# An RWKV-7 core in four steps: key products moved inside each level, level 0 of the inverse taken as a masked copy of L

## The reference, cut to what matters

```
def step(state, inp):                       # wkv7_scan, inside lax.scan
    r_t, w_t, k_t, v_t, a_t, b_t = inp
    sa = jnp.einsum('bhvk,bhk->bhv', state, a_t)
    state = state * w_t[:, :, None, :] + sa[..., None] * b_t[:, :, None, :] + v_t[..., None] * k_t[:, :, None, :]
    y = jnp.einsum('bhvk,bhk->bhv', state, r_t)
    return state, y
y_f, bonus_f = direction(0); y_b, bonus_b = direction(1)
y = y_f + y_b
```

## Time and profile before

| what | value |
|---|---|
| median of three executions | 1351.7 us |
| the profiled execution, its own time | 1352.12 us |
| its span in the profile | 1350.0 us |
| PE busy | 1307.8 us, 97% |
| PEld busy | 999.6 us, 74% |
| DVE busy | 883.9 us, 65% |
| ACT busy | 351.5 us, 26% |
| POOL busy | 120.7 us, 9% |
| granted clock of TensorE, mean | 0.995 |

### The profile page before, as it was taken

The page is one execution under the profiler, slowest core; times in us unless marked ns, Lnnn a source line. Parts: engine busy times, 40 slices in busy tenths (PEclk is TensorE's granted clock), DMA queues, the critical chain, the costliest instruction groups (busy, mean ns, idle before and its releaser), DMA issues.

```text
span 1350.0 us, 25515 instructions
## 1 busy us (share of the span) xinstructions
PE 1307.8 (97%) x11020; PEld 999.6 (74%) x11020; DVE 883.9 (65%) x1486; ACT 351.5 (26%) x756; POOL 120.7 (9%) x184
## 2 busy tenths in 40 slices
PE   7999999999999998999999999998989999999999
PEld 6868649599995444579997467846777765999943
DVE  4577762567878347558898577558444464798973
ACT  2311211212221024413332013703432341233300
POOL 5755000000000001010000000031000000000000
PEclk9989999999999999999999999999999999999999
DMA  8433252334544624044544533400011043354452
GB/s 328 157 133 133 109 187 99 130 126 169 187 162 158 251 84 156 0 179 165 188 165 155 214 153 125 187 1 3 4 35 34 21 170 125 126 188 175 146 184 88
DMA packets 16736, 182.34 MB, mean 135 GB/s; under 512 B 1648, under 2 KB 3952, under 8 KB 6000
## 3 DMA queue, kind: packets, MB, share of 16 engines
q1 hardware_dynamic: 14320, 175.12, 34.9%
q10 hardware_dynamic: 2304, 5.59, 1.1%
HBM read 179.65 MB, written 1.05 MB: 134 GB/s over the span
## 4 chain that ended last, share of the span: by engine, by line
PE 93%; DVE 4%; issue 1%; ACT 1%; DMA 0%; POOL 0%; DVEq 0%; POOLq 0%
PE banks L1722 28%; PE banks L1739 15%; PE banks L1432 11%; PE banks L1399 10%; PE banks L1409 4%; PE banks L2037 3%; PE banks L2026 2%; PE banks L1616 2%; PE banks L1687 2%; PE banks L1385 2%; DVE weight_ring L3140 1%; PE banks L2172 1%; PE banks L1881 1%; PE banks L2044 1%; DVE arena L3140 1%
## 5 line engine op out<-in xcount | busy, mean ns | idle before, releaser
L1722 PE MATMUL banks<-xn,arena 128*128 128x128 f32 x1440 | 165.7, 275 | 0.0
L1722 PEld LDWEIGHTS banks<-xn,arena 128*128 128x128 f32 x1440 | 163.2, 192 | 0.0
L1739 PE MATMUL banks<-arena 128*128 128x512 f32 x264 | 122.0, 592 | 0.0
L1722 PE MATMUL banks<-hT,weight_ring 128*128 128x128 f32 x960 | 116.5, 275 | 0.0
L1722 PEld LDWEIGHTS banks<-hT,weight_ring 128*128 128x128 f32 x960 | 111.8, 192 | 0.0
L1432 PE MATMUL banks<-weight_ring,arena 128*128 128x512 f32 x224 | 97.8, 593 | 0.8 <-ACT arena L1322 0.8
L1739 PEld LDWEIGHTS banks<-arena 128*128 128x128 f32 x264 | 49.8, 190 | 60.7 <-issue 60.7
L1739 PE MATMUL banks<-weight_ring,arena 128*128 128x512 f32 x198 | 93.3, 592 | 0.0
L2733 DVE SCALAR_TENSOR_TENSOR arena<-arena,prm 128x255 f32<-128x255 f32 x200 | 87.3, 479 | 5.4 <-ACT arena L1076 3.6
L1432 PEld LDWEIGHTS banks<-weight_ring,arena 128*128 128x128 f32 x224 | 42.2, 190 | 51.4 <-issue 49.7
L1076 ACT ACTIVATE arena<-arena,prm 128x256 f32<-128x256 f32 x100 | 54.6, 593 | 86.3 <-issue 44.2
(11 more groups left out here) (455 smaller groups left out, 2188.4 us busy)
## 6 DMA issues: line engine op xcount, KB each, us to landing
weight_ring<-in_wall SPq DMA_DIRECT2D x81, 2048.0 KB, 7.5
weight_ring<-in_wall SPq DMA_DIRECT2D x2, 1024.0 KB, 7.3
x<-in_x_tok ACTq DMA_DIRECT2D x2, 512.0 KB, 4.5
arena<-in_mem_tok SPq DMA_DIRECT2D x1, 1024.0 KB, 17.3
arena<-in_wall SPq DMA_DIRECT2D x1, 1024.0 KB, 5.1
arena<-in_wide SPq DMA_DIRECT2D x2, 512.0 KB, 5.1
out_y<-x ACTq DMA_DIRECT2D x4, 256.0 KB, 2.0
arena<-in_masks ACTq DMA_DIRECT2D x1, 896.0 KB, 9.6
```

Source lines behind the costliest of these rows:

```text
L1722: ins = mm(b_(n)[:, j * P:(j + 1) * P], lhsT=weights[:, kb, j * P:(j + 1) * P], rhs=features_[:, kb, :], start=opens and j == 0 and kb == ...
L1739: ins = mm(b_(n), lhsT=a, rhs=b, start=pair == 0, stop=pair == FB // 2 - 1)
```

## The change

In steps 1 to 3, level 0 is no longer computed by TensorE. VectorE writes the masked L directly into the turned T (`Tt`, set to the identity by GpSimd) with eight predicated copies of 64 x 256, TensorE turns it (`tw`) and ScalarE evicts the result into Tc. Level 1 then has no `tt`. The key products ab{j}1.. move from behind `tl` to between `yl` and `tl` of levels 1 to 3 (the fourth behind `tl` of level 4, in step 3 of level 3). VectorE copies `tl` of that level ahead of that product. `s_out` moves into level 4 between `yl` and `tl`; y_out(2,0) and gate(0) likewise in step 3. One product of the following step goes between `yl` and `tl` of level 5, in step 0 too, the other stays behind `tl`. The two `bk` pieces of a step go to levels 0 and 1 of the next one, gate(1) to level 0 of step 3. The core of the diff:

```
+def level_opens(j, lv):
+    return [(f"{x}{j}{lv}{h}", 1, "pair") for x in (("tt",) if lv > 1 else ()) + ("yl",) for h in HALVES]
+def level_closes(j, lv):
+    return [(f"tl{j}{lv}{h}", 1, "pair") for h in HALVES]
+def later_step(j, lv):
+    if lv == 0:
+        out = turned_keys(j - 1, 0) if j < 3 else [("gate1", 1, "pair")]
+        return out + tail_groups(j - 1, "xs") + [(f"tw{j}{h}", 1, "pair") for h in HALVES]
+    opens, closes, keys = level_opens(j, lv), level_closes(j, lv), key_products(j, 1, 0) + key_products(j, 1, 2)
+    if lv < 4:
+        out = opens + [keys[lv - 1]] + closes + [keys[3]] * (j == 3 and lv == 3) + tail_groups(j - 1, TAIL_AT[lv])
+        return out + (turned_keys(j - 1, 1) if lv == 1 and j < 3 else [])
+    if lv == 4:
+        y0, y1 = tail_groups(j - 1, "ys")
+        if j == 3:
+            return opens + [y0] + closes + [y1]
+        return opens + tail_groups(j - 1, "ss") + closes + [keys[3], y0] + key_products(j + 1, 0, 0) + [y1]
+    if j == 3:
+        return opens + [("gate0", 1, "pair")] + closes + [("ty1", 1, "pair")]
+    one, two = key_products(j + 1, 0, 2)
+    return opens + [one] + closes + [two]
...
+            def first_level(j, h):                                   # VectorE
+                d = STEPS[j][0]
+                dve.wait_ge(t_identity, 2 * j + h + 1)
+                for pp in range(2):
+                    dve.wait_ge(*when_read(G[f"ab{j}0{h}{pp}"]))
+                L = heads(LA[d][h])
+                m0 = MSK_DIR * (1 - d) + 512
+                for swap in (0, 1):
+                    for r in (0, 1):
+                        mask = masks[SIDE[r], m0:m0 + HD].unsqueeze(1).to_broadcast([HD, 4, HD])
+                        ins = V.copy_predicated(Tt[h][SIDE[r ^ swap], r], mask, L[SIDE[r], 4 * swap:4 * swap + 4, 0, SIDE[r ^ swap]])
+                ins.then_inc(first_level_made, 1)
...
+                    if j == 0 or lv:                                 # VectorE's list
+                        level(j, lv)
+                    if j and 0 < lv < 4:
+                        products(j, 1, (lv - 1) // 2, (lv - 1) % 2)
+                    if j < 3 and lv == 5:
+                        products(j + 1, 0, 1, 0)
...
+            def first_turn(j, h):                                    # TensorE
+                n = G[f"tw{j}{h}"]
+                free(n)
+                pe.wait_ge(first_level_made, 2 * (j - 1) + h + 1)
+                turn(n, Tt_rows[h])
...
+                    level_opens(j, lv)                               # TensorE's list
+                    if j and 0 < lv < 4:
+                        products(j, 1, (lv - 1) // 2, (lv - 1) % 2)
...
+                    if j < 3 and lv == 5:
+                        products(j + 1, 0, 1, 0)
...
+                    level_closes(j, lv)
...
-                    pool.wait_ge(psum_full, G[f"tf{j - 1}{h}"] + 1)
-                    g.tensor_copy(Tc[h], unit).then_inc(t_identity, 1)
+                    pool.wait_ge(psum_full, G[f"tl{j - 1}{LEVELS - 1}{h}"] + 1)
+                    g.tensor_copy(Tt[h], unit).then_inc(t_identity, 1)
```

More of the change, by code:

```diff
@@ L150 @@
-TAIL_AT = {0: "xs", 1: "u1", 2: "x2", 3: "u2", 4: "ys", 5: "ss"}
-def core_pieces(j, lv):
-    out = []
-    if lv < 4:
[L157 to L170, removed]
+TAIL_AT = {1: "u1", 2: "x2", 3: "u2"}
@@ new lines, in turned_keys, with first_step @@
+def turned_keys(j, i):
+    return [(f"bk{j}{i}", 1, "pair")]
+def first_step(lv):
+    opens, closes = level_opens(0, lv) if lv else [], level_closes(0, lv)
+    if lv == 1:
+        opens = [("tt01%d" % h, 1, "pair") for h in HALVES] + opens
+    if lv < 4:
+        return opens + closes + key_products(0, 1, lv // 2 * 2)[lv % 2:][:1] + [("tx_bonus", 1, 7)] * (lv == 2)
+    if lv == 4:
+        return opens + closes + key_products(1, 0, 0)
+    one, two = key_products(1, 0, 2)
+    return opens + [one] + closes + [two]
@@ L1296, in level, with keys_turned, gate_out @@
                     evict_pair(Yb[h], G[f"yl{j}{lv}{h}"])
+            def keys_turned(j, i):
+                n = G[f"bk{j}{i}"]
+                act.wait_ge(psum_full, n + 1)
+                act.wait_ge(second_keys, 1)
+                out = r_bk.rearrange("p (a k c) -> p a k c", a=2, k=KB)[:, :, 4 * i:4 * i + 4, :]
+                A(out, pair_(n).rearrange("p a (k c) -> p a k c", k=4), ACT.Copy).then_inc(bank_sem(n), 1)
+            def gate_out(tt):
+                n = G[f"gate{tt}"]
+                act.wait_ge(psum_full, n + 1)
+                A(gate_t[:, tt * D:(tt + 1) * D].rearrange("p (b n) -> p b n", b=2), pair_(n), ACT.Copy).then_inc(bank_sem(n), 1)
             def tail(j, piece):
@@ L1326, in _ @@
                     level(j, lv)
-                    if j and lv < 4:
-                        tail(j - 1, TAIL_AT[lv])
[L1329 to L1340, removed]
+                    if j and lv == 0:
+                        if j < 3:
+                            keys_turned(j - 1, 0)
+                        else:
+                            gate_out(1)
+                        for h in HALVES:
+                            evict_turned(Tc[h], G[f"tw{j}{h}"])
+                        tail(j - 1, "xs")
+                    if j and 0 < lv < 4:
+                        tail(j - 1, TAIL_AT[lv])
+                    if j in (1, 2) and lv == 1:
+                        keys_turned(j - 1, 1)
                     if (j, lv) == (3, 5):
+                        gate_out(0)
                         y_tokens(1)
@@ L2045, in turn, with left, level_opens @@
                 ins.then_inc(psum_full, 1)
-            def unit(r, swap, k):
-                return ident[SIDE[r], SIDE[r]]
             def blocks(ap):
                 return lambda r, swap, k: ap[SIDE[r], r ^ swap, k]
[L2055 to L2077, removed]
+            def left(j, h):
+                L = heads(LA[STEPS[j][0]][h])
+                return lambda r, swap, k: L[SIDE[r], 4 * swap + k, 0, SIDE[r ^ swap]]
+            def level_opens(j, lv):
+                for h in HALVES if lv > (j > 0) else ():
                     n = G[f"tt{j}{lv}{h}"]
@@ L2244, in _ @@
                             x_finish(j - 1, h)
[L2245 to L2251, removed]
-                        for pp in range(2):
-                            products(j + 1, 0, lv - 4, pp)
-                    if (j, lv) in GATE_AT:
-                        gate(GATE_AT[j, lv])
+                    if j in (1, 2) and lv == 4:
+                        y_out(j - 1, 0)
+                    if j < 3 and lv == 4:
+                        for pp in range(2):
+                            products(j + 1, 0, 0, pp)
+                    if j and lv == 4:
+                        y_out(j - 1, 1)
+                    if j in (1, 2) and lv == 1:
+                        tokens_of_keys(j - 1, 1)
+                    if j < 3 and lv == 5:
+                        products(j + 1, 0, 1, 1)
                     if (j, lv) == (0, 2):
@@ L3237, in _ @@
                                       b3(n, TT, P).rearrange("p t (q c) -> p t q c", q=4)[:, :, :, 0:4]).then_inc(bank_sem(n), 1)
[L3238 to L3242, removed]
+                    if j in (1, 2) and lv == 4:
+                        y_sum(j - 1, 0)
+                    if j < 3 and lv == 4:
+                        if j == 0:
+                            dve.wait_ge(kept_zero, 2)
+                        for pp in range(2):
+                            products(j + 1, 0, 0, pp)
+                    if j and lv == 4:
+                        y_sum(j - 1, 1)
+                    if j < 3 and lv == 5:
+                        products(j + 1, 0, 1, 1)
                     if (j, lv) == (3, 4):
```

91 lines of the change are left out of this document (65 added, 26 removed).

## The result

The changed kernel took 1372.58 us in the median of four executions (1369.75 to 1379.72), the kernel before 1352.06 (1350.8 to 1353.76). The ratio is 1.0154, interval 1.0134 to 1.0174: 20.5 us slower, where 9.5 slower was forecast. The profiled execution is the slowest of the four, 1379.72 us (span 1377.6), so its own difference to the profiled execution before is 27.6 us. Its mean granted clock is 0.978, the other three have 0.984; the profiled execution before has 0.995, and so, within 0.001, have all 58 executions of that kernel beside the experiments.

What follows compares the result with a forecast made beforehand. PE, busy for 97% of the span, was taken as the bound. Costs of 26.8 us less savings of 16.6 gave 10.2 slower, a level-by-level clock 9.2; 9.5 was taken, forecasting 1361.2 us, range 1354 to 1367.

Steps and rivals of the forecast that it cites:

- What goes: PE time saved in the steps: level 0 matmuls 5.6 us, waits 9.6, overlap of instruction ends 1.4, together 16.6 us.
- The chain of a recycled pair: Levels 1, 3, 5: PE waits for a pair until DVE copies `tl`, then the product; nine waits of 2.2, 19.9 us.
- `tt` behind `x2`: Level 2: `x2` has fixed banks and covers 1.1 us; the next `tt` waits 1.1, three times, 3.4 us.
- The 0.5 of `tt` for the fourth product: Step 3 level 4: `tt` waits for the copy of the fourth product, 0.5 us.
- Small terms: Added costs: `yl` waiting for `tw` 1.2 us, `bk` uncovered in step 1 1.0, DVE's level 0 copies late 0.8.
- The eight copies: DVE's masked copies for level 0: 3.5 us taken, between 2.4 and 5.6.
- `yl` behind `tw`: Level 1: `yl` waits for ScalarE to evict `tw`, 0.4 us three times, 1.2 us.
- `tw` behind the copies: Level 0: DVE's eight copies end 0.4 us late for the second `tw` in steps 1 and 2, 0.8 in all.
- The `bk` piece out of step 0: Step 0 level 4: removing it saves nothing, PE stands for DVE's two products anyway; it costs 1.0 us in step 1.
- Behind the steps everything shifts with PE.: Tail: DVE's normalising slack of 4.5 us shrinks to 3, weight loads have more, so only PE's shift counts.
- The sum at full clock: Whole change: 26.8 us come, 16.6 go, 10.2 slower; worked level by level 9.2; 9.5 taken.
- rival C: Nine levels: clock falls to 1.2 GHz once in each, doubling 2 us of work, 18 us, 1379; chance 0.06.

Runs made afterwards that it cites:

- The skipped pair: Changed kernel, VectorE's order kept, one bank pair skipped behind `tl` in levels 1, 2, 3 and 5: 1347.3 us, ratio 0.9953 to the kernel before.

## Why the prediction was wrong

The direction, the place and the chain of waits were right. The sum had no term for the clock, and that was more than half of the loss: 9.5 us forecast, 20.5 measured, the range ended at 1367. The steps of the prediction in turn.

- **What goes.** Right. The 0.3 waits of `tl` went from 16 to none, level 0's 64 matmuls are gone three times. Of the masked level 0 alone the runs show 3.5 us.
- **The chain of a recycled pair**, "3.3 us from T", nine waits of 2.2, 19.9 us: measured 3.32 and 2.1 to 2.2, 19.3 in all. `tt` behind `x2`: 3.4 forecast, 3.2 measured. The 0.5 of `tt` for the fourth product did not show in this profile, where the pieces before it ran at the low clock; with the waits filled it was 0.3. The skipped pair and the product copied first both confirm it.
- **Small terms.** The eight copies were taken as 3.5 us and lasted 3.66; `yl` behind `tw` 1.2 forecast, 1.0 measured. `tw` behind the copies, 0.8 forecast, is hidden in this profile by slow pieces and was 0.5 with the waits filled. Each copy lasts 0.44 and the next starts 0.46 after it (3.66 / 8), so they do not lap; this agrees with the held start that the Trainium skill states for a change of side (VectorE: DVE Perf Modes, "Two Vector instructions with no wait between them").
- **The `bk` piece out of step 0.** "Saves nothing there" is right for the idle time: the piece of 1.0 goes and the stand grows from 0.82 to 1.83. That the longer stand could cost the clock was not asked; the first fall of the changed kernel is behind it.
- **"Behind the steps everything shifts with PE."** Wrong in one place: I looked at DVE's chain and its 4.5 us of slack, not at ACT's list, where the eviction of `xs` stands behind the square. The wait there was 0.64 before and 1.16 after. As idle time that is 0.5 us. The whole stretch took 17.3 us before, 24.8 after, and 18.1 in the kernel that copies the product first, at full clock, so here too most of the difference is the clock.
- **The sum at full clock.** Forecast 9.5, measured 7.7 with the waits filled; for the steps alone 9.2 and 7.0. Right within 2.2 us, of which 1.1 are three small terms (`tt` for the fourth product, `yl` behind `tw`, which was 0.6 there, and `tw`).
- **The step that failed: the clock, put at nothing in the sum and left to rival C, "The clock falls".** C was named, with its place and a price of 18 us, and given 0.06. The argument for the low chance was that the old steps stayed at 1.00 with up to 0.5 of idle per group; but that says nothing about waits four times as long. The row that did show a longer wait, 1.92 us at 538.43 with the slow matmuls right behind it, spoke for C. I had put that fall down to how empty the whole stretch around it was, not to the wait. In the profiles the clock fell behind 17 of 21 open waits of 2.0 to 2.2 us and behind none of 24 filled ones. Its share is 12 to 13 us of 20.5. The price of 18 was too high: nine falls in the steps cost 11.5, 1.3 each in place of 2. The Trainium skill's section that I set aside (TensorE: Matmul & The Clock Gate, "A second HAM failure mode: psum-queue depth-cycling": short idle times between groups that cycle through PSUM make the clock swing) was the better guide; the windows at 0.89 agree with it.

The forecast missed a sum of both, 9.5 and some 12: C was not a rival to the waits but their second price.

## What to carry to other kernels

When work is moved ahead of a barrier to fill a gap, check whose buffers it holds and where its reader stands in the reader's list: with a few buffers in strict turn, the piece that reuses them inherits the whole queue of the reader. Copy out first what was produced first, unless the next buffer user is far away. And price a new wait on TensorE twice, as idle time and as the clock that may fall behind it. Here the nine waits were 19.3 us of idle time, and the falls in the steps cost another 11.5, more than the 7.0 that the rearranged order cost net at full clock.

## What the runs showed of the hardware that was not expected

- Idle waits of 2.15 us, nine between 948 and 1087 us, were followed by a granted clock that fell to 0.50 for a part of each stretch, 0.89 in its mean over 60 us; the same program with these waits filled by matmuls whose result is never used stood at 1.00 there and was 11.5 us faster (by the ratios 1.0154 and 1.0069). Work whose result nobody reads paid for itself.
- The fall is not the same in each execution: of eight of the kernel that copies the product first, the one with a mean clock of 0.995 took 1342.88 us, that with 0.987 took 1351.52. In the profiled one (0.994) the clock stood at 0.97 over 940 to 1000, behind a single wait of 1.83 us. The 58 executions of the kernel before beside these runs all showed 0.994 to 0.996.
- A 128 x 128 by 128 x 512 f32 matmul of constants is recorded as two and took 0.92 us in all (six in 2.77).
